# A state space layer inside the paged steps of a stick-breaking attention stage, behind a compressed prompt, with two steps' pages and the small tables loaded during the projection

## The reference, cut to what matters

```python
def even_mixer(x, sb_past, ssm_h0, w_in, w_out, ...):
    q, k, v, u = jnp.split(x @ w_in, [SB_WIDTH, 2 * SB_WIDTH, 3 * SB_WIDTH], axis=-1)
    ...
    a_out = stick_breaking_attention(q, k_all, v_all, sb_bias).reshape(Bsz, L, SB_WIDTH)
    b_out, h_last = s5_ssm(u, lam_re, lam_im, log_dt, b_re, b_im, c_re, c_im, d_skip, w_glu, ssm_h0)
    out = jnp.concatenate([a_out, b_out.astype(a_out.dtype)], axis=-1) @ w_out
def stick_breaking_attention(q, k, v, bias):
    # z = q k / sqrt(d) + bias;  w_j = sigmoid(z_j) * prod over later keys of sigmoid(-z);  out = w v
def s5_ssm(u, ...):
    # h_t = a h_(t-1) + B u_t (complex);  y = Re(C h) + d u;  y = gelu(y);  y = y * sigmoid(y @ w_glu)
```

## Time and profile before

| what | value |
|---|---|
| time, median of 3 runs | 3624.64 us (3620.97 to 3629.15) |
| span of the profiled execution, first to last instruction | 3627.8 us |
| PE busy | 3458.0 us (95%) |
| DVE busy | 1930.8 us (53%) |
| ACT busy | 1185.3 us (33%) |
| POOL busy | 618.2 us (17%) |

### The profile page before, as it was taken

The page is one execution under the profiler, slowest core; times in us unless marked ns, Lnnn a source line. Parts: engine busy times, 40 slices in busy tenths (PEclk is TensorE's granted clock), DMA queues, the critical chain, the costliest instruction groups (busy, mean ns, idle before and its releaser), DMA issues. The chain is left out here.

```text
span 3627.8 us, 66971 instructions
## 1 busy us (share of the span) xinstructions
PE 3458.0 (95%) x25890; PEld 2914.0 (80%) x25890; DVE 1930.8 (53%) x3018; ACT 1185.3 (33%) x2527; POOL 618.2 (17%) x686
## 2 busy tenths in 40 slices
PE   8999999998889999999999999799978999999998
PEld 8987777776668999888897777466767899988887
DVE  3148877785766444444446566456077634444435
ACT  2137666665131211111125454321243211111112
POOL 0001111221002211111112111047021211111113
PEclk9999999999989999999999999899978999999999
DMA  4159999998030111111121100069333111111112
GB/s 145 50 210 399 405 415 413 415 413 322 14 121 12 47 47 46 46 46 36 45 85 73 47 30 26 23 219 340 108 95 100 35 47 46 46 46 46 35 46 73
DMA packets 188699, 472.88 MB, mean 130 GB/s; under 512 B 31553, under 2 KB 129717, under 8 KB 152582
## 3 DMA queue, kind: packets, MB, share of 16 engines
q1 hardware_dynamic: 168630, 449.64, 33.4%
q10 hardware_dynamic: 19824, 19.92, 1.7%
HBM read 449.60 MB, written 19.91 MB: 129 GB/s over the span
## 5 line engine op out<-in xcount | busy, mean ns | idle before, releaser
L2089 DVE TENSOR_TENSOR x<-x,f_d 128x512 f32<-128x512 f32 x540 | 367.9, 686 | 292.0 <-PE f_d L1882 249.5
L2062 POOL TENSOR_TENSOR f_hl<-f_h,f_hh 128x364 fp32r<-128x364 f32 (+1 forms) x192 | 181.1, 944 | 1243.6 <-ACT f_hh L2005 1243.5
L2107 DVE TENSOR_TENSOR f_h<-f_h 128x364 f32<-128x364 f32 (+1 forms) x192 | 106.5, 557 | 513.3 <-ACT f_h L1999 513.3
L1882 PE MATMUL f_d<-f_w2h,f_hl 128*128 128x512 f32 x896 | 354.4, 396 | 0.0
L1882 PE MATMUL f_d<-f_w2l,f_hh 128*128 128x512 f32 x896 | 354.4, 396 | 0.0
L1882 PE MATMUL f_d<-f_w2h,f_hh 128*128 128x512 f32 x896 | 354.3, 395 | 0.0
L1999 ACT ACTIVATE f_h<-up 128x364 f32<-128x364 f32 (+1 forms) x192 | 90.6, 473 | 537.5 <-PE up L1752 528.9
L1752 PE MATMUL up<-xH,w1h 128*128 128x364 f32 (+1 forms) x768 | 252.9, 329 | 2.1 <-ACT f_h L1999 2.1
L1752 PE MATMUL up<-xL,w1h 128*128 128x364 f32 (+1 forms) x768 | 252.2, 328 | 0.0
L1752 PE MATMUL up<-xH,w1l 128*128 128x364 f32 (+1 forms) x768 | 252.2, 328 | 0.0
L1752 PE MATMUL up<-xH,f_w1l 128*128 128x364 f32 (+1 forms) x768 | 252.2, 328 | 0.0
(11 more groups left out here) (615 smaller groups left out, 7939.7 us busy)
## 6 DMA issues: line engine op xcount, KB each, us to landing
x<-in_cache_sb_kv SPq DMA_DIRECT2D x256, 512.0 KB, 6.3
ss_kv<-in_cache_sb_kv SPq DMA_DIRECT2D x256, 512.0 KB, 6.3
w<-in_ffn_w SPq DMA_DIRECT2D x64, 1024.0 KB, 5.2
mp_qb<-mp_q SPq DMA_DIRECT2D x24, 1024.0 KB, 8.4
mp_vc<-in_cache_dil_kv ACTq DMA_DIRECT2D x9, 1024.0 KB, 5.6
pe_raw<-in_w_in_even SPq DMA_DIRECT2D x8, 1024.0 KB, 8.0
mp_kc<-in_cache_dil_kv SPq DMA_DIRECT2D x8, 1024.0 KB, 11.3
group_w<-in_w_in_odd SPq DMA_DIRECT2D x3, 2048.0 KB, 10.3
```

The lines of the kernel that those rows point to most:

```text
L1882: mm = pe.matmul(out, a, b, start=(n == 0), stop=(n == len(parts) - 1))
L2062: low = lambda dst, n0, n1, at: g.tensor_tensor(dst, h[:, u % HSLOTS, n0 - at:n1 - at], hh[:, c % 2, f, n0:n1].bitcast(F32), ALU.subtract)
L2089: v.tensor_tensor(K.x[0:r, t, cs], K.x[0:r, t, cs], dn_b[(c * DOWN + u) % 4][0:r, :], ALU.add).then_inc(added, 1)
L2107: v.tensor_tensor(x, x, x, ALU.mult).then_inc(squared, 1)
```

## The change

The stage state_space is gone. Its work is the class SpaceStage, whose engine programs are generators; the steps of stick_both call each of them twice per step from SPACE_STEP = 82 on (94 calls to the end). To make room, prompt_ticks packs the 122 ticks left into 82 steps (41 of them take two ticks, 41 one), where before they took 122. Further:

- E is built by GpSimd from step 30 on; padded weights and output weights are made by GpSimd, quarter by quarter, once the prompt is done, as products of five instructions: two on 64 partitions x 512, one on 128 x 512, two on 64 x 512.
- SpaceStage has three PSUM banks (those of the prompt) and the key banks for the final states. The eight (tile, part) products of the chunk states go in groups of 3, 3 and 2 instead of 4 and 4.
- The C and h0 rows are loaded before step 4's pages and transposed in ten of the two-tick steps (turn_rows, keep_rows).
- I.load and space.load stand ahead of the v stores; the pages of steps 0 and 1 are issued at the end of turn_and_project.

```diff
+                I.load(sp)
+                space.load(sp)
                 for t in range(TT):
                     store(t, "v")
...
-                I.load(sp)
-                space.load(sp)
+                sp.wait_ge(turned, 2 * TT)
+                I.pages(sp, 0)
+                sp.wait_ge(done, last[6])
+                I.pages(sp, 1)
...
+def prompt_ticks(count):
+    steps, t = [], AHEAD
+    while t < count:
+        both = len(steps) % 4 in (1, 2) and t % 2 == 1
+        steps.append((t, t + 1) if both else (t,))
+        t += len(steps[-1])
+    return steps
...
-                for g in range(NSTEP):
+                for g in range(2, NSTEP):
                     if g >= SLOTS:
                         sp.wait_ge(S["pv_done"], g - SLOTS + 1)
+                    if g == SLOTS:
+                        factors.load(sp)
                     I.pages(sp, g)
-                sp.wait_ge(p_out, NB)
-                factors.load(sp)
+                stage.sync(sp)
...
                 for g in range(NSTEP + 1):
-                    t = tick(g)
+                    due = at_step(g)
                     if g < NSTEP:
                         turn_keys(g, 0)
                         turn_keys(g, 1)
-                    if t - 2 < NU:
-                        prompt_turn(t - 2)
+                    if due and due[0] - 2 < NU:
+                        prompt_turn(due[0] - 2)
+                    if g >= ROWS_STEP and due and due[0] % 2 == 1 and row_blocks_turned < factors.ROWS:
+                        factors.turn_rows(pe, zp[0], row_blocks_turned, p_read, due[0])
+                        row_blocks_turned += 1
+                    if g >= SPACE_STEP:
+                        next(space, None)
                     if g < NSTEP:
                         turn_keys(g, 2)
                         turn_keys(g, 3)
                     if g >= 1:
                         turn_weights(g - 1)
...
+                    if due:
+                        prompt_products(due[0])
+                    if len(due) == 2:
+                        if due[1] - 2 < NU:
+                            prompt_turn(due[1] - 2)
+                        prompt_products(due[1])
+                    if g >= SPACE_STEP:
+                        next(space, None)
                     if g == 0:
                         turn_new()
                     if g >= 1:
...
                 gather(DB // 2 - 1)
+                for _ in space:
+                    pass
+                stage.finish_tensor(pe)
```

TensorE's generator, each yield one call, q = 0 with five empty calls ahead and behind:

```diff
+            turn(q, 0)
+            yield
+            turn(q, 1)
+            turn(q, 2)
+            yield
+            turn(q, 3)
+            yield
+            yield
+            first, second, third = [(A, 0, 0, 0), (B, 0, 2, 0), (C, 1, 1, 1)], [(A, 1, 1, 0), (B, 1, 3, 0), (C, 0, 0, 1)], [(A, 2, 2, 1), (B, 2, 3, 1)]
+            states(q, first, 0)
+            yield
...
+            couple(q, 1).then_inc(S["kd"], 1)
+            yield
...
+                yield from all_taps(q - 1)
+                yield from outputs(q - 1)
+        yield from all_taps(3)
+        yield from outputs(3)
```

More of the change, by code:

```diff
@@ new lines, in rows_at, with turn_rows @@
+        self.h0 = alloc("s5f_h0", [P, 2, SJ, DB], F32, offset=place + 4 * 2 * SJ * NCH)
+        self.cS = alloc("s5f_cS", [P, 2, SJ, SC], F32, offset=at)
+    ROWS = 10
+    def turn_rows(self, pe, bank, n, read, units):
+        pe.wait_ge(read, units)
+        if n == 0:
+            pe.wait_ge(self.c_loaded, 64)
+        if n < 8:
+            mm = pe.transpose(bank[:, 3 * P:4 * P], self.cn[:, n // 4, n % 4].rearrange("p a b -> p (a b)"), self.K.ident[:, :])
+        else:
+            pe.wait_ge(self.h0_loaded, 16)
+            for j in range(8):
+                at = 3 * P + j * 2 * DB
+                mm = pe.transpose(bank[:, at:at + 2 * DB], self.h0n[:, 8 * (n - 8) + j, :], self.K.ident[0:2 * DB, 0:2 * DB])
+        mm.then_inc(self.turned, 1)
@@ new lines, in all_taps, with outputs @@
+        def all_taps(q):
+            taps(q, 0, (0, 1, 2))
+            yield
+            taps(q, 1, (0, 1))
+            yield
+            taps(q, 1, (2, 3, 4, 5))
+            yield
+            taps(q, 2, (0, 1, 2, 3))
+            yield
+            taps(q, 2, (4, 5, 6, 7)).then_inc(S["tapped"], 1)
+            yield
+        def outputs(q):
+            pe.wait_ge(S["Hn"], q + 1)
+            pe.wait_ge(S["ca"], q + 1)
+            pe.wait_ge(S["Hset"], 2 * q + 3)
+            for n, (t0, nt) in enumerate(LAGS):
+                for t in range(nt):
+                    for r in range(2):
+                        for jj in range(4):
+                            lo = 2 * SC * jj
+                            mm = pe.matmul(self.banks[n][lo:lo + 2 * SC, t * NC:(t + 1) * NC], CA[:, r, t0 + t, jj, :],
+                                           H[:, r, jj, :], start=False, stop=(t == nt - 1 and r == 1), skip_group_check=True)
+                mm.then_inc(S["yd"], 1)
+                yield
@@ new lines, in tensor @@
+        for _ in range(self.IDLE):
+            yield
+        prompt_done(pe)
+        for q in range(4):
+            turn(q, 0)
+            yield
+            turn(q, 1)
+            turn(q, 2)
+            yield
+            turn(q, 3)
+            yield
+            yield
+            first, second, third = [(A, 0, 0, 0), (B, 0, 2, 0), (C, 1, 1, 1)], [(A, 1, 1, 0), (B, 1, 3, 0), (C, 0, 0, 1)], [(A, 2, 2, 1), (B, 2, 3, 1)]
+            states(q, first, 0)
+            yield
+            states(q, first, 1).then_inc(S["xd"], 1)
+            yield
+            pe.wait_ge(S["xd"], 3 * q + 1)
+            states(q, second, 0)
+            yield
+            states(q, second, 1).then_inc(S["xd"], 1)
+            yield
+            yield
+            pe.wait_ge(S["xc"], 5 * q + 3)
+            states(q, third, 0)
+            yield
+            states(q, third, 1).then_inc(S["xd"], 1)
+            yield
+            couple(q, 0)
+            yield
+            couple(q, 1).then_inc(S["kd"], 1)
+            yield
+            if q == 0:
+                for _ in range(self.IDLE):
+                    yield
+            else:
+                yield from all_taps(q - 1)
+                yield from outputs(q - 1)
```

838 lines of the change are left out of this document (459 added, 379 removed).

## The result

The changed kernel takes 3677.4 us (median of 4 runs, 3674.6 to 3680.9), the kernel before 3625.6 us beside it (3621.0 to 3629.2): ratio 1.0148, 95% interval 1.0136 to 1.0160. Some 52 us slower, where 11 us less was forecast. The profiled execution has a span of 3679.1 us against 3627.8, so the two traces show the same 51.3 us.

A forecast was written before the change was run, and what follows sets the result against it. PE was taken to bound the steps, DMA nearly as long; -105.4 + 93.5 + 3.6 - 3.0 = -11.3 us took 3624.6 to 3613 us. Own range 3600 to 3626, overall range 3594 to 3645.

The forecast's parts named there:

- What goes: Between last gather and gate: 111.2 us now, 5.8 stay, so 105.4 us disappear.
- What PE takes in: State space pieces moved into PE's paged steps count in full: 90.4 us plus 3.1 for cuts, +93.5.
- rival 1: Dearer pieces on PE, no gain: cuts at 0.2 us, two-tick steps at 0.3, total 3631 us; chance 0.20.
- rival 3: More gain: groups of three cost at most 0.17 us, cuts nothing, new waits half; 3593 us, chance 0.13.
- Waits: PE's idle in the steps: 14.9 us saved, 18.5 new, net +3.6, ends -8 and +22.
- VectorE behind step 82: Where PE's state space calls are empty, VectorE is late by 1 to 2 us: 5 us in all.
- The old wait for the weights' copy: PE waits for ScalarE's copy again in 12 empty calls at 0.47 to 0.55 us, 10 at 0.2: 7.5.
- my sign of being wrong: Behind step 82: wrong if VectorE or ScalarE releases most of PE's idle time.
- The loads: Earlier tables and first pages: first keys sooner, -3.0 us (ends -1 and -4); delayed weight slab costs 0.
- rival 2: GpSimd's product chain too slow, PE waits for weights: 41 us at 3.1 us a product, 3654 us; chance 0.13.
- rival 4: Paged steps are bound by DMA, moved work is free, steps stay 5.1 us: 3516 us; chance 0.04.
- Rival 5: State space calls left over would run behind the steps; 94 yields match 94 calls, so no chance of its own.

The follow-up runs named there:

- e8: e6 without GpSimd's products for the padded and output weights (state space outputs wrong): 3624.4 us, ratio 1.0004.
- e11: The kernel before with only the change's packing of prompt ticks, the state space stage left behind the steps: 3709.6 us.
- e3: The changed kernel without GpSimd's 80 late products for padded and output weights (state space outputs wrong): 3657.0 us.
- e2: The changed kernel with VectorE's keep of the prompt values ahead of the prompt's scan in two-tick steps: 3656.6 us.
- e6: Changed kernel; in two-tick steps second turn behind the step's values, ScalarE's weights copy ahead of the prompt sigmoids, VectorE's keep ahead of the scan: 3644.2 us.
- e4: The changed kernel with the small tables' loads and the first two steps' page loads moved back to their later places: 3681.1 us.

## Why the prediction was wrong

**The bound** was read rightly: PE, with DMA close behind. e8 confirms it from the other end: PE is busy 96 and 97% of its two stretches there, up to the last gather, and moving its work gains nothing. e11 shows the DMA close behind.

**What goes** (105.4): 105.6 measured, from the end of the last gather as in the forecast. From the last gather to the gate, timeline of all engines of the changed kernel:

```profile
1058.14 0.39 PE L593 MATMUL ss_zw<-si_sel,ss_newacc 128*128 128x64 f32 x2
...
1064.13 0.73 DVE L1691 TENSOR_TENSOR gp_sq<-uT 128x544 f32<-128x544 f32 x1 [5.35 <-PEq L85]
```

5.6 us from the gather's end (1058.53), 5.8 forecast.

**What PE takes in** (93.5 with 3.1 for the cuts): 92.6, cuts included. Taps 33.9 (33.5), chunk states 27.1 (23.9), outputs 15.8 (16.7), transposes of weights 8.3 (7.3), coupling 5.4 (6.3), rows 2.1 (2.7). The sum is nearer than its terms: the states were too low, the outputs, the coupling and the rows too high, and that they cancel is luck. The states show what a cut costs in this shape. A call of four groups of three takes 1.14 us, a call of four groups of two 1.13 (start to start of the next keys, timeline of PE):

```profile
774.87 0.39 PE L1551 MATMUL ss_zp<-uT,s_bT 32*128 32x136 f32 x2
...
776.01 1.09 PE L549 MATMUL ss_tk<-ident,x 128*128 128x128 f32 x8
...
787.21 1.20 PE L1551 MATMUL ss_zp<-uT,s_bT 32*128 32x136 f32 x16
...
788.34 1.09 PE L549 MATMUL ss_tk<-ident,si_kv1b 128*128 128x128 f32 x8
```

A group is two passes over its tiles. Passes inside a call start 0.116 us apart (timeline of PE, 775.09 to 775.79), the first and the last take 0.22, so a cut costs 0.2 there, rival 1's price and not my 0.05; the passes themselves were a little cheaper than I took them. A group of three took 0.285 us with its share of the cut, so rival 3's 0.17 is out. The Trainium skill's TensorEngine Tiling (Array Packing), section "Key Properties", has a change of tiling mode drain TensorE; the trace is in line with it.

**What I had not in the sum at all** are the 19.1 us by which the steps' and the prompt's own pieces grew. I wrote that the sum over PE stays. One part is the clock. From the first keys to the last gather the granted clock misses 12.3 us of full clock, where the kernel before misses 3.9 on the same way, so up to 8 us: "its low clock" did not vanish with the stage, part of it came back where waits lay close together. The window with the largest loss has PE at 14.65 of 20 us:

```profile
800.00:820.00 20.00, 14.65 (x189) 10.46 (x190) 18.48 (x32) 7.34 (x17) 10.68 (x8) 0.83 0.82 287
```

The clock fell to 1.2 GHz at 804.5 there, behind the wait of 1.72 us (802.52) and during that of 1.98 (806.49). The other 11 or so have no shown cause. They do not go when the waits and most of the clock's loss are cured (13.5 are left in e8, 10.8 in e3). They lie in the two-tick steps (a turn ahead of the prompt's scores takes 0.41 us on the mean, one ahead of keys 0.29 before; prompt values 0.72 instead of 0.68) and behind step 82. State space pieces as new neighbours are not needed for most of it: in e11, which has none in its steps, the same pieces grew by 17.1. A part may lie in the count, since a piece ahead of an idle stretch is counted to its modelled end: up to the last gather PE has 52 idle stretches before, 112 in the changed kernel and 157 in e11. None of this was tried apart.

**Waits: the step that failed.** The prediction's "0.1 each, 4 (up to 0.5 each, 20)" for the two-tick steps was 40.6 us in 39 steps, 1.04 each, twice my upper end. I had asked whether ScalarE and GpSimd could turn two units round, and they could. I had not asked which bank the second turn writes and who must have read it. The term was sized by the engines' load; it is set by a write after a read in `ss_to` and by the place of the keep in VectorE's queue. e2 halves it, e6 removes it. The second failed term is VectorE behind step 82: 5 forecast, 16.9 measured (8.0, 7.8 and three small ones). The old wait for the weights' copy was 3.3 instead of 7.5 and the instruction supply 1.3 instead of 2, so the three together were 14.5 forecast and 21.5 measured. All idle of PE behind step 82, short stretches too, is 22.2 us, and 10.2 without GpSimd's products. So my sign of being wrong came true: VectorE releases most of PE's idle time behind step 82. With both causes cured PE's idle is 25.3 us in e8, where my sum had 22.4 + 3.6 = 26.0. My net term for waits was right for a kernel without these two, in its sum and partly by luck: 17.6 us of that idle lie ahead of the 83rd weighing, where I had booked savings and the kernel before has 10.3. Such a kernel still takes 3624 us and not 3613; the difference is about what the own pieces grew.

**The loads** (-3.0): right by the traces. First keys at 227.03, 3.0 earlier; undoing it costs 3.6 in e4, which is not clear of noise. Slab 4 went out at 82.70 (83 to 86 forecast), ScalarE split it at 89.99 instead of 84.48, and PE did not wait between 84 and 112: the cover held.

**GpSimd** (rival 2): its price per product was as I took it, 1.17 to 1.49 us with the stretch (p of 1.26 to 1.5), and PE never stood for a padded weight (0.2 us ahead of L1543, released by VectorE). The rival's mechanism did not decide; its "for" did, by another road. A slow GpSimd was not the trouble but a GpSimd that reads. The 4.5 us that the prediction takes from the Trainium skill's GPSIMD Engine Reference, section "Elementwise", stand there for an add of two operands, not for a product. The estimate of 1.12 us scaled from it is near the 1.06 us that the undisturbed 128x512 products took here.

**The other rivals.** Rival 1 named the right place (two-tick steps at 0.3) and not the size. Rivals 3 and 4 are out: steps of the packed stretch took 6.28 us on the mean and those behind 6.71, where rival 4 had 5.1. PE was busy 90 and 92% where I asked for 95. Rival 5: 6 us between gather and gate, so the calls ended with the steps.

**The range** of 3594 to 3645 missed by 32 us: its upper end held cases one by one, and what happened was two at once, the larger of them outside its own bound.

## What to carry to other kernels

When two units of a pipeline are put in one step, list each buffer that both write and find who reads it in between and what stands ahead of that reader in its queue; the load of the engines does not show it. After curing such a wait look again before counting the gain: three queue orders stood in a row here; two of them gave 9 and 21 us alone, the three together 33. Work given to an idle GpSimd is not free for VectorE; count how many of VectorE's instructions have two SBUF operands and stand on the critical chain, and prefer to give GpSimd what only writes, or reads little.

## What the runs showed of the hardware that I had not expected

- VectorE's 128x257 scan took 0.752 us alone and beside GpSimd memsets, 0.780 on the mean beside copies and 0.906 beside products; single ones 1.85. Its 128x512 products (16 in four lines) took 0.68, 0.68, 0.84 and 1.07 on the mean, those of the line stretched most 0.684, 0.687, 0.995 and 1.440. GpSimd's own 128x512 products took 1.06 to 1.54 us in the changed kernel.
- A pass of 136 columns over two or three 32-row tiles starts 0.116 us behind the one before it, and so does one over four tiles in the kernel before (timeline of PE, from 932.10): a tile that is left out saves no time.
- The granted clock fell (0.83 over 20 us) in the middle of otherwise full steps, where PE was busy 14.65 of 20 us and none of its waits was longer than 1.98 us.
